# A two-block transformer kernel: adaLN modulation moved from TensorE to VectorE, first projections accumulated by chunk

## The reference, cut to what matters

```python
s_lat, s_ctx = silu(c), silu(c_ctx)
sh1, sc1, g1, sh2, sc2, g2 = split(s_lat @ w_mod + b_mod, 6)
csh1, csc1 = split(s_ctx @ w_mod + b_mod, 6)[:2]
h  = rms_norm(x, norm1_g) * (1 + sc1) + sh1
hc = rms_norm(ctx, norm1_g) * (1 + csc1) + csh1
x = x + g1 * token_mixers(h, hc, ..., w_in, ...)      # attention, differential attention, Hyena
h = rms_norm(x, norm2_g) * (1 + sc2) + sh2
x = x + g2 * conv_glu(h, w_up, ffn_conv_w, ffn_conv_b, w_down)
```

## Time and profile before

| what | value |
|---|---|
| times of three runs | 2184.49, 2186.86, 2190.71 us (median 2186.86) |
| span of the profiled execution | 2185.2 us, 1.7 below that median (the profile gives no other time of its own) |
| PE busy | 2132.4 us (98%), weight loads 1911.0 |
| DVE / ACT / POOL busy | 1249.6 / 479.7 / 546.3 us |
| bytes moved | 609.01 MB, mean 279 GB/s |
| granted TensorE clock, mean | 0.993 of full |

### The profile page before, as it was taken

The page is one execution under the profiler, slowest core; times in us unless marked ns, Lnnn a source line. Parts: engine busy times, 40 slices in busy tenths (PEclk is TensorE's granted clock), DMA queues, the critical chain, the costliest instruction groups (busy, mean ns, idle before and its releaser), DMA issues.

```text
span 2185.2 us, 32173 instructions
## 1 busy us (share of the span) xinstructions
PE 2132.4 (98%) x13288; PEld 1911.0 (87%) x13288; DVE 1249.6 (57%) x2503; ACT 479.7 (22%) x1103; POOL 546.3 (25%) x430
## 2 busy tenths in 40 slices
PE   7999899999999999999999999999999999999999
PEld 4466688888678999999999998678999999999998
DVE  2345521123654798889644444662988889744444
ACT  3114310002241224444100000251223544100000
POOL 0000000000000074454433332000064555443332
PEclk9999999999999999999999999999999999999999
DMA  9325053444424498999999997323498999999997
GB/s 388 135 77 211 11 193 130 159 160 167 154 97 154 155 382 338 386 376 411 396 409 409 409 409 302 147 114 135 159 367 326 387 375 401 404 409 409 408 409 280
DMA packets 112252, 609.01 MB, mean 279 GB/s; under 512 B 9961, under 2 KB 11369, under 8 KB 94058
## 3 DMA queue, kind: packets, MB, share of 16 engines
q1 hardware_dynamic: 56394, 403.31, 47.8%
q0 software_dynamic: 55424, 201.55, 23.5%
q10 hardware_dynamic: 288, 2.10, 0.3%
HBM read 605.77 MB, written 1.15 MB: 278 GB/s over the span
## 4 chain that ended last, share of the span: by engine, by line
PE 83%; DVE 9%; DMA 6%; issue 1%; ACT 1%; SPq 0%; ACTq 0%; DVEq 0%
PE psum L428 81%; DMA arena<-in_peer_v 5%; PE psum L488 2%; DVE arena L2057 1%; DVE arena L2096 1%; DVE arena L2090 1%; DVE arena L2055 1%; DMA KON<-in_consts 1%; DVE arena L2060 1%; PE psum L536 1%; DMA arena<-in_w_up 0%; DVE arena L2100 0%; DVE arena L1647 0%; DVE arena L1659 0%; DVE arena L2075 0%
## 5 line engine op out<-in xcount | busy, mean ns | idle before, releaser
L428 PE MATMUL psum<-arena 128*128 128x160 f32 (+5 forms) x6386 | 978.8, 315 | 8.9 <-DMA arena<-in_peer_v 3.3
L428 PEld LDWEIGHTS psum<-arena 128*128 128x128 f32 (+1 forms) x6386 | 902.4, 190 | 67.0 <-issue 30.9
L428 PE MATMUL psum<-HT,arena 128*128 128x160 f32 (+1 forms) x5472 | 874.5, 320 | 4.4 <-ACT HT L1204 3.4
L428 PEld LDWEIGHTS psum<-HT,arena 128*128 128x128 f32 x5472 | 822.8, 191 | 41.5 <-issue 4.1
L2167 DVE SCALAR_TENSOR_TENSOR arena<-arena,small 128x1024 f32<-128x1024 f32 x180 | 231.3, 1285 | 291.7 <-DMA arena<-in_peer_v,small 291.4
L2291 POOL DMA_INDIRECT arena<-in_peer_u,small x192 | 249.7, 1301 | 286.7 <-DVE small L2118 171.5
L2291 POOL DMA_INDIRECT arena<-in_peer_v,small x192 | 219.7, 1144 | 356.1 <-PE psum L428 287.8
L2302 POOL TENSOR_TENSOR arena<-arena 128x512 f32<-128x512 f32 x12 | 15.4, 1286 | 826.4 <-ACT arena L1233 826.1
L2118 DVE CUSTOM_DVE_ANT_0 arena<-arena 128x1024 f32<-128x1024 f32 x168 | 198.5, 1220 | 0.7 <-DVE arena L2142 0.6
L428 PE MATMUL psum<-arena,HT 128*128 128x384 f32 (+3 forms) x544 | 196.0, 518 | 1.3 <-ACT HT L1120 0.8
L428 PEld LDWEIGHTS psum<-arena,HT 128*128 128x128 f32 x544 | 104.1, 194 | 84.2 <-issue 35.9
(11 more groups left out here) (246 smaller groups left out, 1100.3 us busy)
## 6 DMA issues: line engine op xcount, KB each, us to landing
arena<-in_peer_ut SPq DMA_DIRECT2D x64, 2048.0 KB, 10.4
arena<-in_peer_v SPq DMA_DIRECT2D x64, 2048.0 KB, 17.2
arena<-in_w_mod SPq DMA_DIRECT2D x12, 2048.0 KB, 8.9
arena<-in_w_in SPq DMA_DIRECT2D x16, 1536.0 KB, 6.1
arena<-in_w_up SPq DMA_DIRECT2D x11, 2048.0 KB, 7.9
arena<-in_peer_wq SPq DMA_DIRECT2D x8, 2048.0 KB, 7.4
arena<-in_w_out SPq DMA_DIRECT2D x6, 2048.0 KB, 7.5
arena<-in_w_down SPq DMA_DIRECT2D x11, 1024.0 KB, 4.9
```

What stands on the lines that cost most here:

```text
L428: return pe.matmul(o, a, b, start=start, stop=stop, skip_group_check=True)
```

## The change

The table is transposed on the host and cut by output: each of the 48 chunks of 128 outputs is a 128 x 1024 tile (output on the partition), four to a 2 MB load, ordered scale, shift, scale, shift for the first eight tiles of chunks (`MOD_CHUNKS`). The silu'd conditions are spread over all partitions once (`DIAG` on DVE, ones matmuls `conditions` on PE, `CB`). Then one DVE multiply-and-sum gives 128 outputs with the bias added (`modulation_dots`). Tiles 0 to 3 are also done for the context: 64 such operations in all. Tiles 0 to 7 land in areas `MA` of their own, 8 to 11 still pass through the ring. The order of DVE is (tile, condition): (0,0) (0,1) (1,0) (1,1) (2,0) (3,0) (2,1) (3,1), then 4, 5, 6, 7; tiles 8 and 9 one operation in each attention item 1 to 8, tiles 10 and 11 after `gate` in FFN steps 3 and 5. Gain and shift are applied by ACT in one operation per chunk (`modulated`). PE accumulates the first two token projections by pairs of chunks as they come; f1, f2, f3 and the context projections move behind; `zc4` now comes after `zx4`. All `modulation_rows`, `modulation_columns`, their copies and adds go away.

```diff
-            modulation_rows(2)
-            modulation_rows(3)
-            square_sums("ssx", 0)
...
+            conditions(0)
+            conditions(1)
+            square_sums("ssx", 0, (s("x_squared"), 0))
+            in_tiles[0] = in_weights(0)
+            latent_part(0, 0)
+            in_tiles[1] = in_weights(1)
+            for j in range(1, 4):
+                latent_part(0, j)
+                if j == 1:
+                    latent_part(1, 0)
+                latent_part(1, j)
+            in_tiles[2] = in_weights(2)
+            latent_job(2, 0)
+            square_sums("ssc", 1, (s("ctx_squared"), 0))
+            latent_job(2, 1)
             filter_1()
...
+            in_tiles[3] = in_weights(3)
+            latent_job(3, 0)
             filter_2()
...
+            latent_job(3, 1)
+            in_tiles[4] = in_weights(4)
+            filter_3()
+            context_job(2)
+            filter_sum()
+            context_job(3)
+            filter_spectra()
+            for b in range(TB):
+                latent_job(4, b)
+            context_job(4)
...
-                if i % 3 == 0 and MODS_BEFORE_ATTENTION + i // 3 < MODS_BEFORE_FFN:
-                    modulation_rows(MODS_BEFORE_ATTENTION + i // 3)
...
             for f in range(2, FC // 2):
+                if f in (3, 5):
+                    modulation_weights(10 if f == 3 else 11)
                 up(f)
                 down(f - 1)
...
+                for c in chunks:
+                    m, done = MOD_CHUNKS[4 * tile + c], dots_done(tile, which, c)
+                    w = mod_tile(tile)[:, c * D:(c + 1) * D]
+                    dump = w
...
+                    dve.tensor_tensor_reduce(out=dump, in0=w, in1=CB[which], scale=1.0,
+                                             scalar=col("bmod", m), op0=ALU.mult, op1=ALU.add,
+                                             accum_out=MOD[:, m, which:which + 1]).then_inc(s("mod_dots"), 1)
+                    if m < KC:
+                        dve.wait_ge(s("mod_dots"), done - 1)
+                        dve.tensor_scalar(AMP[:, which, m:m + 1], MOD[:, KC + m, which:which + 1], 1.0,
+                                          col("n1g", m), ALU.add, ALU.mult).then_inc(s("amp_ready"), 1)
...
+            modulation_dots(2, 1)
+            mean_square("ssc", 1)
+            modulation_dots(3, 1)
+            inverse_stream(1)
+            for g in range(4):
+                scaled_pair(1, g)
+            modulation_dots(4, 0)
             sine_argument(1, "fb1")
...
+            modulation_dots(5, 0)
             dve.wait_ge(s("sine_out"), 1)
             sine_argument(2, "fb2")
...
+            modulation_dots(6, 0)
+            modulation_dots(7, 0)
...
+            filter_windows()
...
                 if n == 4:
...
+                    modulation_load(4)
+                    modulation_load(5)
+                    modulation_load(6)
+                    sp.wait_ge(s("mod_dots"), dots_done(0, 1))
+                    load(GAIN, ins["gains_1"], "gain_in")
+                    modulation_load(7)
+                    sp.wait_ge(s("mod_dots"), dots_done(6, 0))
                     load(FW3[0:65, :], ins["hy_fw3"], "windows_in")
                     load(DECAY[:, :, :], ins["decay"], "windows_in")
                     load(DFT[:, :, :, :], ins["dft"], "windows_in")
```

More of the change, by code:

```diff
@@ L87, in gated_before, with dots_done @@
     return min(GBATCHES, max(0, -(-(m - FIRST_GATED) * GBATCHES // slots)))
+def dots_done(tile, which, chunk=3):
+    return 4 * MOD_STEPS.index((tile, which)) + chunk + 1
 def pairs_before(n):
@@ L528, in filter_spectra @@
                         end(last, f"kf{part}{fb}")
[L530 to L539, removed]
@@ new lines, in modulation_weights, with conditions @@
+            def modulation_weights(tile):
+                ring_mods[tile] = len(loads)
+                loads.append({"src": ins["w_mod"][tile], "width": WSIZE, "n": len(loads),
+                              "last": (s("mod_dots"), dots_done(tile, 0))})
+            def conditions(which):
+                pe.wait_ge(s("diagonal"), which + 1)
+                for half in range(2):
+                    ps = begin(f"cb{which}{half}")
+                    end(mm(ps[:, :], ONES, DIAG[:, which, half * 512:(half + 1) * 512], True, True),
+                        f"cb{which}{half}")
@@ L589, in _ @@
[L589 removed]
+                tile, w = in_weights(len(IN_TILES) + t)
                 for j in range(3):
@@ L1125, in shifted @@
                     last.then_inc(s("h_ready"), 1)
+            def shifted(dst, first):
+                for k in range(KC):
+                    act.wait_ge(s("normed"), k + 1)
+                    if k % 4 == 0:
+                        act.wait_ge(s("mod_dots"), dots_done(8 + k // 4, 0))
+                    act.activation(dst[:, k, :], dst[:, k, :], ACT.Identity, bias=MOD[:, first + k, 0:1]
+                                   ).then_inc(s("h_ready"), 1)
             def head_squares():
@@ new lines, in modulation_dots @@
+            def modulation_dots(tile, which, chunks=range(4)):
+                if 0 in chunks:
+                    if tile in MOD_AREA:
+                        area = MOD_AREA[tile]
+                        before = sum(MOD_AREA[n] == area for n in range(tile))
+                        dve.wait_ge(mods_in[area], 16 * (before + 1))
+                    else:
+                        n = ring_mods[tile]
+                        dve.wait_ge(weights_in[n % WSLOTS], 16 * (n // WSLOTS + 1))
+                for c in chunks:
+                    m, done = MOD_CHUNKS[4 * tile + c], dots_done(tile, which, c)
+                    w = mod_tile(tile)[:, c * D:(c + 1) * D]
+                    dump = w
+                    if tile < 4 and which == 0:
+                        dump = SQF[:, 2048 + c % 2 * D:2048 + (c % 2 + 1) * D]
+                    if done > 2:
+                        dve.wait_ge(s("mod_dots"), done - 2)
+                    dve.tensor_tensor_reduce(out=dump, in0=w, in1=CB[which], scale=1.0,
[5 more added lines that the diff above has]
+                                          col("n1g", m), ALU.add, ALU.mult).then_inc(s("amp_ready"), 1)
@@ L1800, in _ @@
                 gate(f - 1)
+                if f in (3, 5):
+                    modulation_dots(10 if f == 3 else 11, 0)
             gate(FC // 2 - 1)
-            jobs.wait_read(dve, "mod11")
+            dve.wait_ge(s("mod_dots"), dots_done(11, 0))
             for n in range(4):
@@ L2351, in stream, with modulation_load @@
                 sp.dma_start(dst, src).then_inc(weights_in[n % WSLOTS], 16)
-            load(CS[:, :, :], ins["c"], "params_in")
+            def modulation_load(tile):
+                area = MOD_AREA[tile]
+                if tile >= 4:
+                    before = max(n for n in range(tile) if MOD_AREA[n] == area)
+                    sp.wait_ge(s("mod_dots"), dots_done(before, 1 if before < 4 else 0))
+                sp.dma_start(MA[:, area, :], ins["w_mod"][tile]).then_inc(mods_in[area], 16)
+            load(CS[:, :, :], ins["c"], "c_in")
+            load(KON[:, 0:2 * P], ins["consts"][:, 0:2 * P], "ident_in")
+            load(XT[:, :, :], ins["x"], "x_in")
             load(CP[:, :], ins["cols_1"], "params_in")
+            modulation_load(0)
             for n, tile in enumerate(loads):
```

289 lines of the change are left out of this document (146 added, 143 removed).

## The result

| | median, us | runs |
|---|---|---|
| before | 2186.11 | 4, 2184.49 to 2190.71 |
| after | 2216.78 | 4, 2215.74 to 2220.07 |

What follows compares the result with a forecast made beforehand. PE, 83% of the chain, was taken as the bound. Heads 13.2, attention -6, into the FFN -2.5 and FFN ring 5.6 summed to +10.3 us: 2195.5 against the 2185.2 span, forecast as 2197.2; range 2188 to 2210.

Steps and rivals of the forecast that it cites:

- The price of a sum: A DVE multiply-and-sum over 128 x 1024 float32 was put at 1.15 us from start to start.
- The rival in which the sums don't overlap: Each sum takes 1.30 us, so 40 on the path cost 0.15 more each: +6, 2203; chance 0.15.
- Part 1: Up to the last chunk of h: first sum at 20, last chunk at 52, projections end at 57: -0.5 us.
- Part 2: To the end of the Hyena jobs: -5.5 of PE work, waits +2.9 and +9.9, half clock +2; PE ends 8.8 later.
- The sine: Wait of PE for the sine, ready at 85.1 when PE asks at 82.2: +2.9 us.
- the tables: Wait of PE for filter tables, loaded when tile 6 is summed: there at 102.4, PE through at 92.5: +9.9 us.
- +2 (between 0 and 3): PE runs some us at half clock after the pause at the filter tables: +2 us.
- Part 3: The heads: DVE goes on only after copying `zc4`, which now follows `zx4` and ends at 159.2; first scores +13.2 us.
- Part 4: Attention: 8.3 of table tiles leave PE, some 2.5 of DVE sums uncovered: -6 us; bounds -8.3 and +0.9.
- attention gives nothing: Rival for attention: DVE's sums land on PE's path one for one, +0.9 there, time 2204; chance 0.14.
- Part 5: Into the FFN: load is early, the norm's chain ends 0.7 before it did, columns (1.84) go: -2.5 us.
- Part 6: FFN ring: `w_up` waits for table sums or slots, PE waits 2.3 twice and 0.5 twice: +5.6 us (0 to 8).

Runs made afterwards that it cites:

- experiment 2: Changed kernel with PE calls on constants ahead of six waits, 3 and 9 of them at the second and third filter matmul: 2217.41 us.
- experiment 3: Changed kernel with 3 and 12 PE calls on constants ahead of the second and third filter matmul only: 2211.29 us, and 2208.41 us when run again.
- experiment 4: Changed kernel with the two small filter tables loaded when tile 4 is summed, only the DFT table behind tile 6: 2199.97 us.
- experiment 9: Changed kernel with FFN tables off the ring, small filter tables early, zc4 before zx4, both sine arguments early, four PE calls before the FFN: 2173.99 us.
- experiment 6: Kernel before, with the three table tiles 7 to 9 and their columns left out of the attention loop: 2184.31 us, ratio 0.9994.
- experiment 11: Changed kernel with FFN/filter loads and zc4 reordered, sines and token sums early, PE calls on constants before the FFN and three attention items: 2164.8 us.
- experiment 5: Changed kernel without the eight multiply-and-sums of tiles 8 and 9 in the attention items: 2217.25 us.
- experiment 1: Changed kernel with tiles 10 and 11 loaded into free attention areas before FFN step 2, not through the ring: 2204.8 us.

## Why the prediction was wrong, step by step

**The price of a sum** was 1.205 us from start to start (a row lasts 1.28), where 1.15 was taken: 2.2 us more over the 40 sums on the path. The rival in which the sums don't overlap fell:

```profile
18.07 1.28 DVE L1539 CUSTOM_DVE_ANT_0 arena<-arena 128x1024 f32<-128x1024 f32 x1
19.28 0.08 DVE L1539 DVE_READ_ACCUMULATOR2_ANT arena<- 128x1 f32 x1
19.28 1.28 DVE L1539 CUSTOM_DVE_ANT_0 arena<-arena 128x1024 f32<-128x1024 f32 x1
```

The next one starts 0.07 before the row of the last ends. By the line on DRAIN in the Trainium skill, VectorE: DVE Perf Modes, Terms, it could not; here too the measurement speaks against it.

**Part 1 was right**, with two errors against each other: the first sum came at 18.07 (20), and from there the last chunk of h took 33.0 us (32) to 51.06 (52). The last copy of the first two projections starts at 55.93 (57).

**Part 2 had the waits right and the clock too small.** The sine cost 2.87 (+2.9), the tables 8.95 (+9.9), with the tables at 101.93 (102.4). But "+2 (between 0 and 3)" for half clock after such a pause was 1.7 behind the sine and 5.2 behind the tables (experiments 2 to 4). I had taken it from one row, 5.41 against 3.62, a loss of 1.8; behind the longer pause it ran on through the next job. **Part 3** inherits it: `zc4` ends at 162.23 (159.2), and the scores are 16.4 later instead of 13.2. The late `zc4` behaved as told.

The Trainium skill, TensorE: Matmul & The Clock Gate, HAM oscillation, describes stages that start at the low clock again after each wait, and advises to order work so that PE stays busy; experiments 2 to 4 and 9 agree, with 1.7, 5.2 and 2.6 us behind single pauses. The sum should have had such a term at each of the long new waits (2.87, 8.95, 5.70, 4.07, 3.24 and 3.25 us); behind those of 0.73 and 0.84 the FFN step took 14.08, as the first of before did.

**Part 4 left the clock out.** -6 was forecast, -1.2 came. "Three table tiles with columns leave PE: 8.3" took what leaves PE for time won. But the loop has pauses in which PE waits for DVE, and when the tiles leave, the clock falls further there: 0.89 for 0.96. PE is busy only 2.3 us less and idle 1.1 more, so 6.0 of the 8.3 came back as slower rows. Experiment 6 shows the same with nothing added on DVE (2.8 won, at most 3.3 by the times), and the loop that runs at 0.98 is 5.3 shorter than before (experiment 11). The bound "-8.3 if all are covered" had no row for it. The sums, put at 2.5, cost nothing that experiment 5 can show. For this stage the rival "attention gives nothing" (+0.9) came nearer than my -6, but for a reason that experiment 5 refutes: it had the sums one for one on the path.

**Part 5 left the clock out too.** The 1.84 us of columns went, the load was early, and the norm's chain ended the wait, all as told: from the first output matmul to the FFN it took 36.26 us instead of 36.71 (0.45 less, 0.7 told). But where the table tiles 10 and 11 had kept PE at work there was now a pause of 4.07, and 2.6 us of clock behind it. Sum 0 instead of -2.5.

**Part 6 had the mechanism, not the size.** Predicted waits 2.3 twice and 0.5 twice, measured 3.24, 3.25 and 0.73, 0.84, so 8.1 for 5.6. The chain on DVE was a little short, the load was right. From the end of `fa` in step 3 (14.08/2 after 367.32, so 374.36), by these rows and the start at 391.57:

```profile
378.91 1.28 DVE L1539 CUSTOM_DVE_ANT_0 arena<-arena 128x1024 f32<-128x1024 f32 x1 [0.26 <-DVE arena L1867]
...
383.85 0.33 SPq L2435 DMA_DIRECT2D arena<-in_w_up  x1
```

Convolution and gate took 4.55 (3.9), the sums 4.94 (4.6), the load 7.72 (7.4 to 7.9): 17.2, not 16.4. Each long wait was followed by a step of 15.77 instead of 14.08. Of the 12.8 in the FFN that explains 11.4. Experiment 1 shows that the ring is the cause of all of it. By the rows the slow steps alone are 3.4 us; that taking them away would gain as much is not shown, since in experiment 2, which took them away, PE started later after the loads were issued.

The range failed with these: the same mechanism, a pause of PE that costs more than its length, was too small in part 2 and missing in parts 4, 5 and 6, so their errors had one sign, and the top of the range had some 6 us above one slower rival for all of it.

## What to carry to other kernels

Price a new wait of TensorE of some us as its length plus the slow work after it, and look at what filled the pauses before: work that is taken from the engine there can come back in part as a lower clock (of 8.3 us of table tiles, 2.8 were won). When work moves to another engine, the loss lies in the waits that the new order adds (a ring slot held until a sum is done, a table load behind a buffer, a copy that starts a chain later), and each can be taken out alone. Before a difference of 2 us in one trace is put down to an edit, look at what the same stage takes in the traces of kernels that leave it alone.

## What was not expected of the hardware

After a pause of 2.68 us, the work that followed was as slow (22.49 us) as after one of 8.95 (22.60), while after 2.87 us at another place the loss was 1.7. The granted clock says the same: at the tables it is 0.50 to 0.60 up to 112 in both runs, at the sine it is back at 1.00 by 90. Why is not shown. TensorE fed with constants through the whole pause loses nothing: with 24 rows of such work in place of the wait, the same 40 rows took 17.41. And the attention loop, with the same instructions, took 71.19 to 74.80 us in eight traces, at a granted clock of 0.93 to 0.89.
